# Scaling a recurrence's output by its root mean square: eight ScalarE operations one chunk later, or two VectorE operations behind the factor

## The chip, the cores and the metric

The kernel runs on one core of a Trainium2 chip. The metric is the time of one execution on the device, in microseconds (us). Three runs of the kernel before took 2665.38, 2669.21 and 2672.31 us; their median, 2669.21 us, is what the changed kernel is compared with.

## The reference, cut to what matters

One layer of a hybrid encoder: an input projection, a gated delta-rule recurrence over 8 heads of width 128, an attention group beside it, an output projection and a final norm. The sequence has 1024 frames of a new stream and 32 frames of a running one. The change lies in the recurrence and the norm that follows it:

```python
def step(s, xs):
    q_c, k_c, u_c, w_c, g_c, a_c = xs
    v_new = u_c - einsum('bhid,bhdv->bhiv', w_c, s)
    o_c = (einsum('bhid,bhdv->bhiv', q_c * exp(g_c)[..., None], s)
           + einsum('bhij,bhjv->bhiv', a_c, v_new))
    s = s * exp(g_last)[..., None, None] + einsum('bhid,bhiv->bhdv', k_dec, v_new)
    return s, o_c
...
o_g = rmsnorm(o_g, gdn_norm_w)      # per frame and head: o / sqrt(mean(o*o) + EPS) * w
o_g = o_g * silu(z_g)
```

## The kernel before

The program is a row of stages, each a block that all engines enter and leave together: `normalise_inputs`, `project`, `delta_rule` (with `decays`, `prepare` and `recur`), `attend`, and `mix_and_finish`. The change touches `recur` alone.

`recur` goes over NC = 9 chunks of 128 frames, c = 0 to 8; the last (LAST = 8) holds the 32 frames of the running stream, padded to 128. Its tensors have 128 partitions (frames of the chunk) and 8 heads of 128 columns. Work is cut in two halves g of HF = 4 heads, each one PSUM bank of 128x512. Every engine has its own list of instructions, written out by hand in program order, and does them strictly in that order; between engines stand semaphores (`then_inc`, `wait_ge`). So what is late on an engine is late for everything behind it on that engine.

In chunk c the order is, by engine (the names are those of the code):

- TensorE (PE): the keys times the state S (into banks 4 and 5, semaphore value kS); the form product of chunk c+1 from its loaded blocks (Bo, Xd); the triangular matrix times R (yP), which waits for R; the queries times the state (qS); the first peel of chunk c+1; the two products with y, for the new state (dS) and for o (Ay); `turn_out(c-1)`, which transposes the scaled o of the chunk before; the second peel; the transposes of the keys of c+1; the third peel; the transposes of the values of c+1.
- VectorE (DVE): R in eight operations of one head (L1070); a subtraction per peel (L1039); the new state S (L1080); the addition that completes o (L1085); `gated(c-1)`, which multiplies the transposed o by the gate and writes `mix` (L1054); `keys(c+1)` (L1046); in chunks 0 to 2 a share of 60 small operations that invert 32x32 blocks for chunks 4 to 7 (L576, L579); and then a chain for the norm: sum of squares `oss` (L1097), `var` (L1099, L1101), and, behind GpSimd, the factor `orr` (L1105). The next instruction on VectorE is R of chunk c+1.
- ScalarE (ACT): copies of the form product (L971), two copies of y (L1011), the queries' part of o (L998), then `normalise(c-1)`: eight operations of one head that scale o of the chunk before by `orr` (L988), `values(c+1)` into `vs` (L980), and the squares of o(c) (L1020).
- GpSimd (POOL): one power, var to the minus half (L962), and, in the chunks 1 to 6, ten small operations of its own inversion for the last chunk (`invert_steps`, L576 and L579 again), which stand in its list between the power of one chunk and that of the next.
- SyncE's queue (SP) issues the loads of the inputs, blocks and gates two chunks ahead, and the stores of `mix`. The blocks for chunk 4 wait until the inverse that VectorE made in chunks 0 to 2 has gone through DRAM.

o has two buffers, by the parity of c, while `orr`, `rms`, `var` and `oss` have one. Therefore VectorE waits for `normalise(c-1)` (`scaled`) before it writes `orr` of chunk c, and PE's `turn_out` waits for the same semaphore, `tail_s`. The counts by which the waits are written are lambdas: `squared` and `scaled`, and 4 increments of `stat` in each chunk.

Of the kernel before, what the change touches and what calls it, by code (L numbers as in the profile page):

```python
# [7 lines left out]
ACT = mybir.ActivationFunctionType  # L8
AX = mybir.AxisListType

P = 128
# [544 lines left out]
HF = HEADS // 2  # L556
# [248 lines left out]
def recur(nc, a, d, cols, ident, out, eg, egl, neg_eg, kl, root_q, root_k, sq2):  # L805
# [6 lines left out]
    with ExitStack() as ctx:  # L812
# [3 lines left out]
        LAST = PROMPT_TILES  # L816
        ROUNDS = NSUB - 1
        qkv = s.sb("qkv", [P, 2, 3 * HEADS, P])
        gate, mix, aT, Bo, Xd, Yd, V, o = (s.sb(n, [P, 2, HEADS, P]) for n in ("gate", "mix", "aT", "Bo", "Xd", "Yd", "V", "o"))
        S = s.sb("S", [P, 2, HEADS, P])  # L820
        pc, kd, vs, R, y, osq = (s.sb(n, full) for n in ("pc", "kd", "vs", "R", "y", "osq"))
        oss, var, rms, orr = (s.sb(n, [P, HEADS]) for n in ("oss", "var", "rms", "orr"))
# [6 lines left out]
        half = lambda g: slice(HF * g, HF * g + HF)  # L829
# [16 lines left out]
        formed = lambda c, g=1: 2 * (ROUNDS + 1) * c + g + 1  # L846
        peel_at = lambda c, r, g=1: 2 * (ROUNDS + 1) * c + 2 * r + g + 3
        y_at, qe_at = (lambda c, g=1, w=w: 4 * c + 2 * w + g + 1 for w in range(2))
        squared, scaled = (lambda c: 3 * c + 1), (lambda c, g=1: 3 * c + g + 2)
        RA, SA, OA = (lambda c, g=1, w=w: 6 * c + 2 * w + g + 1 for w in range(3))  # L850
        stream = lambda c: 1 if c == LAST else 0
        width = lambda c: DEC if c == LAST else P
# [88 lines left out]
        @block.gpsimd  # L941
        def _(pool):
            for t in (Xd, Yd, Bo):
                pool.memset(t[:], 0.0).then_inc(set_up, 1)
            pool.memset(S[:, 0], 0.0).then_inc(set_up, 1)
            pool.memset(mhalf[:], -0.5).then_inc(set_up, 1)
            pool.wait_ge(set_up, 5)
            pool.wait_ge(consts_in, 32)
            pool.wait_ge(sdiag_in, 16)
            invert_start(pool, sstep, Ls, Xs, below, HEADS)  # L950
            for c in range(NC):
                if 0 < c < 7:
                    invert_steps(pool, sstep, Ls, Xs, tmps, HEADS, 5 * c - 4, 5 * c + 1)
                if c == 6:
                    pool.wait_ge(sstep, INVERTED)
                    pool.tensor_copy(Ys[:].rearrange("p (j i) -> p j i", i=SUB), Xs[:].rearrange("p (i j) -> p j i", j=SUB)).then_inc(ys_turned, 1)
                    pool.wait_ge(V_s, level(6, ROUNDS - 1))
                    pool.memset(Yd[:, LAST % 2], 0.0).then_inc(sample_padded, 1)
                    pool.wait_ge(made, qS(LAST - 2))
                    pool.memset(qkv[:, LAST % 2, :, DEC:], 0.0).then_inc(sample_padded, 1)  # L960
                pool.wait_ge(stat, 4 * c + 3)
                pool.tensor_tensor(rms[:], var[:], mhalf[:], ALU.pow).then_inc(rms_s, 1)  # L962

        @block.scalar
        def _(act):
            def form(c):
                for g in range(2):
                    act.wait_ge(peeled, formed(c, g))
                    if c >= 1:
                        act.wait_ge(peeled, peel_at(c - 1, ROUNDS - 1, g))  # L970
                    act.copy(pc[:, half(g)], bank(g)).then_inc(pc_s, 1)  # L971

            def values(c):
                for g in range(2):
                    act.wait_ge(turned, vT(c, g))
                    if c >= 1:
                        act.wait_ge(rso, RA(c - 1, g))
                    for h in range(HF):
                        k = HF * g + h
                        last = act.activation(vs[:, k], bank(2 + g)[:, h], ACT.Copy, scale=root_k[:, c, k:k + 1])  # L980
                    last.then_inc(vs_s, 1)

            def normalise(c):
                act.wait_ge(stat, 4 * c + 4)
                for g in range(2):
                    for h in range(HF):
                        k = HF * g + h
                        last = act.activation(o[:, c % 2, k], o[:, c % 2, k], ACT.Copy, scale=orr[:, k:k + 1])  # L988
                    last.then_inc(tail_s, 1)

            def queries(c):
                for g in range(2):
                    act.wait_ge(made, qS(c, g))
                    if c >= 2:
                        act.wait_ge(oT, two(c - 2, g))
                    for h in range(HF):
                        k = HF * g + h
                        last = act.activation(o[:, c % 2, k], bank(4 + g)[:, h], ACT.Copy, scale=eg[:, c, k:k + 1])  # L998
                    last.then_inc(yq_s, 1)

            form(0)
            values(0)
            for c in range(NC):
                if c + 1 < LAST:
                    form(c + 1)
                for g in range(2):
                    act.wait_ge(made, yP(c, g))
                    if c >= 1:
                        act.wait_ge(made, Ay(c - 1, g))
                        act.wait_ge(made, dS(c - 1, g))  # L1010
                    act.copy(y[:, half(g)], bank(6 + g)).then_inc(yq_s, 1)  # L1011
                queries(c)
                if c >= 1:
                    normalise(c - 1)
                if c + 1 < NC:
                    values(c + 1)
                act.wait_ge(rso, OA(c))
                if c >= 1:
                    act.wait_ge(stat, 4 * (c - 1) + 1)
                act.activation(osq[:], o[:, c % 2], ACT.Square).then_inc(tail_s, 1)  # L1020
                if c == 2:
                    act.wait_ge(step, INVERTED)
                    act.copy(Y[:].rearrange("p (j i) -> p j i", i=SUB), X[:].rearrange("p (i j) -> p j i", j=SUB)).then_inc(y_turned, 1)
            normalise(LAST)

        @block.vector
        def _(dve):
# [34 lines left out]
            for c in range(NC):  # L1062
                for g in range(2):
                    dve.wait_ge(made, kS(c, g))
                    dve.wait_ge(vs_s, two(c, g))
                    if c >= 1:
                        dve.wait_ge(made, yP(c - 1, g))
                    for h in range(HF):
                        k = HF * g + h
                        last = dve.scalar_tensor_tensor(R[:, k], bank(4 + g)[:, h], neg_eg[:, c, k:k + 1], vs[:, k], ALU.mult, ALU.add)  # L1070
                    last.then_inc(rso, 1)
                if c + 1 < LAST:
                    peel(c + 1, 0)
                for g in range(2):
                    dve.wait_ge(made, dS(c, g))
                    if c >= 1:
                        dve.wait_ge(rso, SA(c - 1, g))
                    for h in range(HF):
                        k = HF * g + h
                        last = dve.scalar_tensor_tensor(S[:, stream(c), k], S[:, stream(c), k], egl[:, c, k:k + 1], bank(6 + g)[:, h], ALU.mult, ALU.add)  # L1080
                    last.then_inc(rso, 1)
                for g in range(2):
                    dve.wait_ge(made, Ay(c, g))
                    dve.wait_ge(yq_s, qe_at(c, g))
                    dve.tensor_tensor(o[:, c % 2, half(g)], o[:, c % 2, half(g)], bank(4 + g), ALU.add).then_inc(rso, 1)  # L1085
                if c + 1 < LAST:
                    peel(c + 1, 1)
                if c >= 1:
                    gated(c - 1)
                if c + 1 < NC:  # L1090
                    keys(c + 1)
                if c + 1 < LAST:
                    peel(c + 1, 2)
                if c < 3:
                    invert_steps(dve, step, L, X, tmp, P, (1, 11, 21)[c], (11, 21, 31)[c])
                dve.wait_ge(tail_s, squared(c))
                dve.tensor_reduce(oss[:], osq[:], AX.X, ALU.add).then_inc(stat, 1)  # L1097
                dve.wait_ge(stat, 4 * c + 1)
                dve.tensor_tensor(var[:], oss[:], sq2[:, c], ALU.mult).then_inc(stat, 1)  # L1099
                dve.wait_ge(stat, 4 * c + 2)  # L1100
                dve.tensor_scalar(var[:], var[:], EPS, None, ALU.add).then_inc(stat, 1)  # L1101
                dve.wait_ge(rms_s, c + 1)
                if c >= 1:
                    dve.wait_ge(tail_s, scaled(c - 1))
                dve.tensor_tensor(orr[:], rms[:], root_q[:, c], ALU.mult).then_inc(stat, 1)  # L1105
            gated(LAST)

        @block.tensor
        def _(pe):
# [45 lines left out]

            def turn_out(c):
                for g in range(2):
                    pe.wait_ge(tail_s, scaled(c, g))
                    if c + 1 < NC:
                        pe.wait_ge(vs_s, two(c + 1, g))  # L1160
                    turn(2, g, o[:, c % 2], oT)
# [1107 lines left out]
```

## Time and profile before

| | |
|---|---|
| median of three runs | 2669.21 us (2665.38 to 2672.31) |
| profiled execution, its own time | 2670.6 us |
| its span, first to last instruction | 2668.7 us |
| busy in the span: PE, DVE, ACT, POOL | 2288.1, 859.0, 657.6, 131.0 us |
| mean granted TensorE clock | 0.924 of full speed |
| `recur`, of that span | from about 1376 to 1678 us |

A row of a timeline gives the start in us from the span's start, the time it took, engine, line, operation, output and inputs, the number of operations merged (x), and in brackets the idle time of that engine before it and what ended it. A row of the operations by line gives count, busy time, mean in ns. Where an engine takes up the next operation while the former is still finishing, the rows overlap by some hundredths of a us.

### The profile page before, as it was taken

The numbers are of one execution on the slowest core, as the hardware profiler recorded it, in microseconds if no ns is written. First come the engines' busy times: TensorE is split into PE (matmuls) and PEld (weight loads), VectorE is DVE, ScalarE is ACT, GpSimd is POOL, SyncE is SP. The second block draws the span as 40 slices with busy tenths as digits, with TensorE's granted clock in tenths as the row PEclk, the third lists the DMA queues.
The fourth block names the chain that finished last, engine by engine and source line by source line (L and its number), as shares of the span: only waits on it lengthen the run. The fifth ranks groups of instructions, "written<-read, shape, count | busy, mean of one in ns | idle before, by whom it ended". The sixth has DMA issues, their size and how long they took to land. (4 is left out here: it accounts for less than half of the span.)

```text
span 2668.7 us, 35422 instructions
## 1 busy us (share of the span) xinstructions
PE 2288.1 (86%) x14534; PEld 2211.0 (83%) x14534; DVE 859.0 (32%) x1495; ACT 657.6 (25%) x1109; POOL 131.0 (5%) x192
## 2 busy tenths in 40 slices
PE   3799999999999999995846587379999977999991
PEld 3799999999999999994646576278998967999991
DVE  4233323332111111101535554445445442122114
ACT  7222222222111111112212333334333332111110
POOL 0000000000000000001331221000000000000000
PEclk8899999999999999996768788679999988999996
DMA  3221222222222222213556362331211124332327
GB/s 132 63 72 57 71 71 72 63 72 72 74 70 71 71 71 72 72 41 87 150 146 129 98 145 49 125 101 33 61 53 41 41 100 130 92 96 75 85 65 292
DMA packets 318743, 232.15 MB, mean 87 GB/s; under 512 B 56205, under 2 KB 299102, under 8 KB 315366
## 3 DMA queue, kind: packets, MB, share of 16 engines
q1 hardware_dynamic: 291750, 182.03, 24.7%
q10 hardware_dynamic: 26912, 49.01, 4.8%
q8 instruction: 55, 0.90, 0.1%
q14 instruction: 26, 0.21, 0.0%
HBM read 159.28 MB, written 67.40 MB: 85 GB/s over the span
## 5 line engine op out<-in xcount | busy, mean ns | idle before, releaser
L432 PE MATMUL proj_acc<-h_hn_hi,proj_w_hi 128*128 128x352 f32 (+1 forms) x2352 | 759.6, 323 | 12.3 <-DVE proj_w_lo L377 12.3
L432 PE MATMUL proj_acc<-h_hn_lo,proj_w_hi 128*128 128x352 f32 (+1 forms) x2352 | 754.7, 321 | 0.0
L432 PE MATMUL proj_acc<-h_hn_hi,proj_w_lo 128*128 128x352 f32 (+1 forms) x2352 | 754.2, 321 | 0.0
L432 PEld LDWEIGHTS proj_acc<-h_hn_hi,proj_w_hi 128*128 128x128 f32 (+1 forms) x2352 | 439.9, 187 | 13.2 <-DVE proj_w_lo L377 12.4
L432 PEld LDWEIGHTS proj_acc<-h_hn_lo,proj_w_hi 128*128 128x128 f32 (+1 forms) x2352 | 440.6, 187 | 0.8
L432 PEld LDWEIGHTS proj_acc<-h_hn_hi,proj_w_lo 128*128 128x128 f32 (+1 forms) x2352 | 439.5, 187 | 0.7
L377 DVE TENSOR_TENSOR proj_w_lo<-proj_w_raw,proj_w_hi 128x2048 fp32r<-128x2048 f32 (+1 forms) x49 | 111.5, 2277 | 588.0 <-ACT proj_w_hi L313 588.0
L2145 PE MATMUL mixo_acc<-mixo_m_hi,outw_w_hi 128*128 128x352 f32 x768 | 250.8, 327 | 35.3 <-DVE mixo_m_lo L2102 33.5
L2145 PE MATMUL mixo_acc<-mixo_m_hi,outw_w_lo 128*128 128x352 f32 x768 | 248.0, 323 | 0.0
L2145 PE MATMUL mixo_acc<-mixo_m_lo,outw_w_hi 128*128 128x352 f32 x768 | 247.6, 322 | 0.0
L2145 PEld LDWEIGHTS mixo_acc<-mixo_m_hi,outw_w_hi 128*128 128x128 f32 x768 | 145.1, 189 | 37.6 <-issue 18.9
L2145 PEld LDWEIGHTS mixo_acc<-mixo_m_lo,outw_w_hi 128*128 128x128 f32 x768 | 145.7, 190 | 0.0
L2145 PEld LDWEIGHTS mixo_acc<-mixo_m_hi,outw_w_lo 128*128 128x128 f32 x768 | 145.2, 189 | 0.0
L352 ACT ACTIVATE proj_act_out<-proj_acc 128x352 f32<-128x352 f32 x72 | 33.4, 464 | 445.9 <-PE proj_acc L432 445.9
L2092 DVE TENSOR_TENSOR mixo_yb<-mixo_back,mixo_xb 128x512 f32<-128x512 f32 (+1 forms) x48 | 23.6, 546 | 263.3 <-PE mixo_back L2132 263.3
L393 DVE TENSOR_SCALAR proj_act_out<-proj_pre,all_cols 128x1059 f32<-128x1059 f32 x24 | 18.5, 773 | 268.5 <-ACT proj_pre L342 268.5
L313 ACT CAST proj_w_hi<-proj_w_raw 128x2048 fp32r<-128x2048 f32 (+1 forms) x49 | 92.9, 1896 | 41.4 <-ACT proj_act_out L352 16.0
L397 DVE SCALAR_TENSOR_TENSOR proj_act_out<-proj_pre,all_cols,proj_act_out 128x1059 f32<-128x1059 f32 x72 | 95.2, 1323 | 10.7 <-DVE proj_act_out L393 3.6
L2040 ACT COPY mixo_yT<-mixo_acc 128x352 f32<-128x352 f32 x48 | 18.8, 460 | 324.0 <-PE mixo_back L2132 313.9
L1899 PE MATMUL mla_oT<-mla_pT,mla_v_tok 128*128 128x128 f32 (+2 forms) x624 | 83.9, 278 | 7.7 <-DVE mla_mix L1783 3.8
L1899 PEld LDWEIGHTS mla_oT<-mla_pT,mla_v_tok 128*128 128x128 f32 (+1 forms) x624 | 76.3, 191 | 13.1 <-issue 11.7
L1117 PE MATMUL rec_b<-rec_R,rec_V 128*128 128x128 f32 x128 | 28.4, 412 | 45.6 <-DVE rec_R L1070 45.6
(290 smaller groups left out, 3074.3 us busy)
## 6 DMA issues: line engine op xcount, KB each, us to landing
proj_w_raw<-in_w_in SPq DMA_DIRECT2D x48, 1024.0 KB, 5.6
outw_w_raw<-in_w_out SPq DMA_DIRECT2D x16, 1024.0 KB, 6.1
scratch_qkv<-proj_act_out ACTq DMA_DIRECT2D x24, 529.5 KB, 2.9
rec_qkv<-scratch_qkv SPq DMA_DIRECT2D x8, 1536.0 KB, 7.7
scratch_gate<-proj_act_out ACTq DMA_DIRECT2D x16, 528.0 KB, 2.7
mixo_m_lo<-scratch_mix SPq DMA_DIRECT2D x12, 704.0 KB, 11.3
norm_x<-in_x_prompt SPq DMA_DIRECT2D x8, 1024.0 KB, 5.0
prep_qk<-scratch_qkv SPq DMA_DIRECT2D x8, 1024.0 KB, 6.2
```

The costliest lines, as they stand in the source:

```text
L313: act.copy(w_hi[:, b, :, 0:n], w_raw[:, :, 0:n]).then_inc(hi_ready, 1)
L352: last = act.activation(act_out[:, b, NW * c:NW * c + NW], acc[b][c][:, 0:NW], ACT.Silu if kind == "gate" else ACT.Copy)
L377: dve.tensor_tensor(w_lo[:, b, :, 0:n], w_raw[:, :, 0:n], w_hi[:, b, :, 0:n].bitcast(F32), ALU.subtract).then_inc(lo_ready, 1)
L393: dve.tensor_scalar(y, pre[:, b, 0:CONV], w[0], None, ALU.mult).then_inc(conv_step, 1)
L397: ins = dve.scalar_tensor_tensor(y, pre[:, b, n:n + CONV], w[n], y, ALU.mult, ALU.add)
L432: last = pe.matmul(acc[b][c][0:n, 0:NW], w[:, b, k, 0:n], h[:, k, cut], start=(k == 0 and x == 0), stop=(k == KT - 1 and x == 2))
L1117: last = pe.matmul(bank(b + g)[:, h], lhsT[:, f], rhs[:, f], start=True, stop=True)
L1899: last = pe.matmul(oT[:, 0:n], v_tok[0:m, b, e], pT[0:m, (g - 3) % 2, P * j:P * j + n], start=(j == 0), stop=(j == len(parts) - 1))
L2040: act.copy(yT[:, NW * c:NW * c + NW], acc[u][c][:, 0:NW]).then_inc(yT_ready, 1)
L2092: dve.tensor_tensor(yb[0:rows, u, t0:t1], back[g % 2][0:rows, 0:P * (t1 - t0)].rearrange("p (t n) -> p t n", n=P), xb[0:rows, u, t0:t1], A ...
L2145: last = pe.matmul(acc[u][c][:, 0:NW], w[:, u, k], h[:, k, cut], start=(k == 0 and x == 0), stop=(k == KT - 1 and x == 2))
```

## The change

The eight ScalarE operations of `normalise` and both its calls go. In their place VectorE, right behind `orr` and still in chunk c, multiplies o in two operations of four heads each, in place, with the factor broadcast along the 128 columns of a head. Before them it waits for its own `orr`. `stat` now counts six increments in a chunk, `tail_s` one, and `turn_out` waits on `stat`. The wait of VectorE for `scaled(c-1)` goes.

```diff
-        squared, scaled = (lambda c: 3 * c + 1), (lambda c, g=1: 3 * c + g + 2)
+        squared, scaled = (lambda c: c + 1), (lambda c, g=1: 6 * c + g + 5)
...
-            def normalise(c):
-                act.wait_ge(stat, 4 * c + 4)
-                for g in range(2):
-                    for h in range(HF):
-                        k = HF * g + h
-                        last = act.activation(o[:, c % 2, k], o[:, c % 2, k], ACT.Copy, scale=orr[:, k:k + 1])
-                    last.then_inc(tail_s, 1)
...
                 queries(c)
-                if c >= 1:
-                    normalise(c - 1)
                 if c + 1 < NC:
                     values(c + 1)
...
-            normalise(LAST)
...
                 dve.wait_ge(rms_s, c + 1)
-                if c >= 1:
-                    dve.wait_ge(tail_s, scaled(c - 1))
                 dve.tensor_tensor(orr[:], rms[:], root_q[:, c], ALU.mult).then_inc(stat, 1)
+                dve.wait_ge(stat, 6 * c + 4)
+                for g in range(2):
+                    dve.tensor_tensor(o[:, c % 2, half(g)], o[:, c % 2, half(g)], orr[:, half(g), None].to_broadcast([P, HF, P]), ALU.mult).then_inc(stat, 1)
...
             def turn_out(c):
                 for g in range(2):
-                    pe.wait_ge(tail_s, scaled(c, g))
+                    pe.wait_ge(stat, scaled(c, g))
```

## Rows read from the trace of the kernel before

**Rows 1.** Timeline of all engines, from the squares of chunk 3 to chunk 4's first products
```profile
1545.92 1.10 ACT L1020 ACTIVATE rec_osq<-rec_o 128x1024 f32<-128x1024 f32 x1
...
1547.06 1.22 DVE L1097 TENSOR_REDUCE rec_oss<-rec_osq 128x8 f32<-128x1024 f32 x1 [2.90 <-ACT rec_osq L1020]
...
1548.31 0.17 DVE L1099 TENSOR_TENSOR rec_var<-rec_oss,gdn_sq 128x8 f32<-128x8 f32 x1
1548.52 0.17 DVE L1101 TENSOR_SCALAR rec_var<-rec_var 128x8 f32<-128x8 f32 x1
1548.77 1.64 POOL L962 TENSOR_TENSOR rec_rms<-rec_var,rec_mhalf 128x8 f32<-128x8 f32 x1 [28.70 <-DVE rec_var L1101]
1550.37 0.58 POOL L576 TENSOR_TENSOR rec_tmps<-rec_Ls,rec_Xs 8x240 f32<-8x240 f32 x1
1550.44 0.54 DVE L1105 TENSOR_TENSOR rec_orr<-rec_rms,gdn_root_q 128x8 f32<-128x8 f32 x1 [1.75 <-POOL rec_rms L962]
1550.90 2.15 DVE L1070 SCALAR_TENSOR_TENSOR rec_R<-rec_b,gdn_neg_eg,rec_vs 128x128 f32<-128x128 f32 x8
1551.03 0.69 POOL L579 TENSOR_TENSOR rec_Xs<-rec_Xs,rec_tmps 8x240 f32<-8x240 f32 x1
...
1552.07 3.78 PE L1117 MATMUL rec_b<-rec_R,rec_V 128*128 128x128 f32 x16 [4.19 <-DVE rec_R L1070]
...
1555.64 3.01 PE L1117 MATMUL rec_b<-rec_S,rec_qkv 128*128 128x128 f32 x16
```

**Rows 2.** Waits of `recur`: waiter, what it waited for, us in total, times, longest
```profile
ACT rec_vs L980 <- PE rec_b L1122: 69.2, 8, 9.5
```

**Rows 3.** Timeline of chunk 5: ScalarE's scaling of o, and PE's transposes of it
```profile
1587.35 2.47 ACT L988 ACTIVATE rec_o<-rec_o,rec_orr 128x128 f32<-128x128 f32 x8
...
1589.60 1.95 PE L1117 MATMUL rec_b<-rec_y,rec_aT 128*128 128x128 f32 x16
...
1591.39 1.04 PE L1122 MATMUL rec_b<-all_ident,rec_o 128*128 128x128 f32 x8
```

**Rows 4.** VectorE operations of this size in `normalise_inputs`: by tile (ns min/median/max), then timeline
```profile
L183 DVE TENSOR_TENSOR h_hn_lo<-norm_hn,h_hn_hi x36: 283/684/694, 20.2 to 79.3; 128x512 f32 x24, 128x512 fp32r<-128x512 f32 x8, 128x128 fp32r<-128x128 f32 x4
...
29.90 1.29 DVE L183 TENSOR_TENSOR h_hn_lo<-norm_hn,h_hn_hi 128x512 f32 x2
```

**Rows 5.** Timeline around the factor of chunk 6, where POOL has nothing behind its power
```profile
1633.22 0.17 DVE L1105 TENSOR_TENSOR rec_orr<-rec_rms,gdn_root_q 128x8 f32<-128x8 f32 x1 [1.75 <-POOL rec_rms L962]
1633.33 2.16 DVE L1070 SCALAR_TENSOR_TENSOR rec_R<-rec_b,gdn_neg_eg,rec_vs 128x128 f32<-128x128 f32 x8
...
1634.51 3.78 PE L1117 MATMUL rec_b<-rec_R,rec_V 128*128 128x128 f32 x16 [5.64 <-DVE rec_R L1070]
```

**Rows 6.** Line L1105, the factor: ns min/median/max over the nine chunks
```profile
L1105 DVE TENSOR_TENSOR rec_orr<-rec_rms,gdn_root_q x9: 166/353/539, 1449.7 to 1670.7; 128x8 f32<-128x8 f32 x9
```

**Rows 7.** Timeline: POOL's second operation behind its power, in chunks 0 and 5
```profile
1449.97 0.25 POOL L579 TENSOR_TENSOR rec_Xs<-rec_Xs,rec_tmps 8x30 f32<-8x30 f32 x1
...
1606.16 0.43 POOL L579 TENSOR_TENSOR rec_Xs<-rec_Xs,rec_tmps 8x130 f32<-8x130 f32 x1
```

**Rows 8.** Timeline, VectorE and PE, R and the form product of chunk 3
```profile
1513.82 2.15 DVE L1070 SCALAR_TENSOR_TENSOR rec_R<-rec_b,gdn_neg_eg,rec_vs 128x128 f32<-128x128 f32 x8
...
1523.53 3.77 PE L1117 MATMUL rec_b<-rec_Xd,rec_Bo 128*128 128x128 f32 x16 [18.01 <-DMA rec_Yd<-scratch_inv]
```

**Rows 9.** Timeline of the end of `recur`
```profile
1670.73 0.17 DVE L1105 TENSOR_TENSOR rec_orr<-rec_rms,gdn_root_q 128x8 f32<-128x8 f32 x1 [1.75 <-POOL rec_rms L962]
1670.93 2.45 ACT L988 ACTIVATE rec_o<-rec_o,rec_orr 128x128 f32<-128x128 f32 x8 [3.71 <-DVE rec_orr L1105]
...
1672.26 2.29 PE L1122 MATMUL rec_b<-all_ident,rec_o 128*128 128x128 f32 x8 [5.98 <-ACT rec_o L988]
...
1674.59 0.75 DVE L1054 SCALAR_TENSOR_TENSOR rec_mix<-rec_b,all_cols,rec_gate 128x512 f32<-128x512 f32 x1 [0.32 <-PE rec_b L1122]
1675.36 0.37 SPq L896 DMA_DIRECT2D scratch_mix<-rec_mix  x1
```

More of the change, by code:

```diff
@@ L960, in _ @@
                     pool.memset(qkv[:, LAST % 2, :, DEC:], 0.0).then_inc(sample_padded, 1)
-                pool.wait_ge(stat, 4 * c + 3)
+                pool.wait_ge(stat, 6 * c + 3)
                 pool.tensor_tensor(rms[:], var[:], mhalf[:], ALU.pow).then_inc(rms_s, 1)
@@ L1018, in _ @@
                 if c >= 1:
-                    act.wait_ge(stat, 4 * (c - 1) + 1)
+                    act.wait_ge(stat, 6 * (c - 1) + 1)
                 act.activation(osq[:], o[:, c % 2], ACT.Square).then_inc(tail_s, 1)
@@ L1097, in _ @@
                 dve.tensor_reduce(oss[:], osq[:], AX.X, ALU.add).then_inc(stat, 1)
-                dve.wait_ge(stat, 4 * c + 1)
+                dve.wait_ge(stat, 6 * c + 1)
                 dve.tensor_tensor(var[:], oss[:], sq2[:, c], ALU.mult).then_inc(stat, 1)
-                dve.wait_ge(stat, 4 * c + 2)
+                dve.wait_ge(stat, 6 * c + 2)
                 dve.tensor_scalar(var[:], var[:], EPS, None, ALU.add).then_inc(stat, 1)
                 dve.wait_ge(rms_s, c + 1)
-                if c >= 1:
-                    dve.wait_ge(tail_s, scaled(c - 1))
                 dve.tensor_tensor(orr[:], rms[:], root_q[:, c], ALU.mult).then_inc(stat, 1)
+                dve.wait_ge(stat, 6 * c + 4)
+                for g in range(2):
+                    dve.tensor_tensor(o[:, c % 2, half(g)], o[:, c % 2, half(g)], orr[:, half(g), None].to_broadcast([P, HF, P]), ALU.mult).then_inc(stat, 1)
             gated(LAST)
```

## The prediction

> **What bounds the kernel now.** I read the page first (busy shares, the 40 slices), then the timeline of all engines in the stretch of the recurrence, then the waits of that stretch, and last single lines and tiles for durations. Over the whole span PE is the busiest engine, but an average says nothing about `recur`, where no engine is busy all the time: what counts there is which wait ends last in each chunk.
>
> The timeline shows that this is the norm's own chain, although the next chunk doesn't need its result [rows 1]. ScalarE squares o until 1547.02. VectorE, idle for 2.90 us until then, sums the squares (1547.06, 1.22 us), does two small operations on `var` (1548.31 and 1548.52), waits for GpSimd's power (1548.77, 1.64 us), and makes the factor `orr` (1550.44). R of chunk 4 stands behind it in VectorE's list and starts at 1550.90. PE has then been idle for 4.19 us, and the row names R as what ended that. So whatever VectorE does between `orr` and R is on the path that sets the end, in each chunk where PE waits for R.
>
> ScalarE has time to spare. Before the values of the next chunk it waits for PE's transposes, 69.2 us in 8 waits, up to 9.5 us [rows 2].
>
> **What is removed.** Eight operations of ScalarE in each chunk, 2.47 us together [rows 3]. They lie between the queries' part of o and the values. In chunk 5 they run from 1587.35 to 1589.82, and PE takes the scaled o at 1591.39, right behind a product that started at 1589.60 and kept it busy. So nobody waits for them, and behind them ScalarE only waits longer for PE [rows 2]. I count their removal as 0, except in the last chunk. The dropped wait of VectorE for `scaled(c-1)` was over long before VectorE came to it: in chunk 5 the scaling ends at 1589.82, and GpSimd's operation that follows the factor of that chunk starts at 1606.16 [rows 3, 7]. So that is 0 as well. `turn_out` waits for a count reached about a chunk earlier: 0. No DMA is added or moved.
>
> **What is added, per chunk.** A wait of VectorE for its own factor, and two operations of 128x512 in place. This pair is not in the trace, but its nearest row is an operation of VectorE with two SBUF inputs of the same size: 684 ns, and two in a row take 1.29 us [rows 4]. The wait for an own result shows between the two operations on `var`: the second starts 0.21 us after the first, which took 0.17, so 0.04 us for the wait [rows 1]. Where nothing interferes, the factor starts at 1633.22, takes 0.17, and R starts 0.11 behind that start, which is 0.06 before the factor's end [rows 5]. With the pair R starts 0.17 + 0.04 + 1.29 - 0.06 = 1.44 us behind the start of the factor, so 1.33 us later. Queued behind it on VectorE are R's eight operations, and PE, then ScalarE's copies of y, wait for these. Nothing later in the chunk gives this back, because all of it follows from R.
>
> **How often this is on the path.** There are eight steps from a factor to the next R, and one of them is covered. In chunk 3 R started at 1513.82, but PE then waited until 1523.53 for the blocks of chunk 4 from DRAM (18.01 us idle, ended by a DMA), with its product of R behind that [rows 8]. Those blocks hang on VectorE's inversion in chunk 2, which ends before the pair of chunk 2. So there the pair costs 0. If the cover were gone it would cost the same 1.33. That leaves 7 x 1.33 = 9.3 us.
>
> **What GpSimd does to the pair.** In chunks 0 to 5 GpSimd goes on with its inversion right behind the power. The factor, the one operation of VectorE with two SBUF inputs there, takes 166 ns at least and 539 at most [rows 6]. The 0.17 belongs to a chunk in which GpSimd has nothing more to do [rows 5], and the 0.54 to one where GpSimd's operation runs from 1550.37 to 1550.95 and the factor ends at 1550.98 [rows 1]. So the factor is held until GpSimd's operation is over. GpSimd's next operation starts at 1551.03, 0.05 us behind the factor's end, and the first of the new pair would start at 1551.02 by the 0.04 above. I take it that VectorE comes first by that little, that GpSimd's second operation then stands waiting, and that it goes in between the two halves of the pair. It holds up the second half by its own length, in the five chunks 0, 1, 3, 4 and 5: the first of the five is 0.25 us, the last 0.43 [rows 7], the longest 0.69 [rows 1], and the sum of the five, with 0.48 and 0.58 for the two not shown, is 2.4 us. The bounds: 0 if GpSimd never gets in, and, if it comes first before both halves, the length of one more of its operations each time (0.59 in chunk 3's case, about 2.2 over the five), so 4.6 us. I take the middle, 2.4, since the factor's own row shows that the wait is real.
>
> The Trainium skill bears on this ("SBUF — State Buffer", section "Who interferes with whom"): a VectorE instruction with two SBUF inputs and a GpSimd instruction that reads SBUF exclude each other, and the one that issues second is blocked until the first ends. The factor's rows agree with it [rows 1, 6]. By that rule alone ScalarE's place for this scaling was the free one, and the pair pays for one or two of GpSimd's operations in each of these chunks, as in the sum or above it. The page doesn't say who is served when both are waiting.
>
> **The end of the stage.** Here the scaling is on the path. After the last factor ScalarE needs from 1670.93 to 1673.38, PE's eight transposes take 2.29 us from 1672.26, and the last of `mix` starts at 1674.59, with its store behind it at 1675.36 [rows 9]. The pair would run from 1670.94 to 1672.23, and GpSimd is idle. PE could start at 1670.94 + 0.68 + 0.04 = 1671.66, so 0.60 us earlier, if it needs the 2.29 us again. If it goes by the second half of o, that is there 1.15 us earlier. I take -0.9.
>
> **Sum.** 9.3 + 2.4 - 0.9 = +10.8 us. The profiled execution took 2670.6 us and would take 2681.4. It lies 1.4 above the median of the runs, so against the median of 2669.2 I predict 2680.0 us.
>
> **Rivals.**
> (a) No clash with GpSimd: VectorE's two halves follow each other without a gap. For it: they stand in VectorE's queue with no wait between them. Against it: the factor is held up in every chunk where GpSimd works on. 9.3 - 0.9 = +8.4, 2677.6 us.
> (b) GpSimd comes first twice. For it: the margin before the first half is 0.01 us, less than these rows can tell. 9.3 + 4.6 - 0.9 = +13.0, 2682.2 us.
> (c) The other side: the pair falls into time in which PE would wait anyway, as in chunk 3. It decides at 1.33 us of slack in R. Then only the end of the stage is left, -0.9 and 2668.3 us, not slower. For it: one step of eight is so [rows 8]. Against it: in the other chunks the row of PE's idle time names R [rows 1, 5], and VectorE is the engine that R stands behind.
> (d) The clock. PE comes back from its idle time slow: the 16 products of R take 3.78 us behind 4.19 idle, and 3.78 behind 5.64 idle [rows 1, 5], while 16 products at full clock take 1.95 [rows 3]. That the longer idle time changes nothing there is in my sum. The next 16, with the queries, took 3.01 [rows 1], between the two. If the added wait shifted them all to slow, each of the seven chunks would lose 3.78 - 3.01 = 0.77, in all +5.4: 2685.4 us. If all came at full clock, 7 x 1.06 = 7.4 would come back: 2672.6 us. I see nothing in the rows that favours a side.
>
> **How the numbers follow.** My forecast 0.45, (a) 0.27, (b) 0.13, (c) 0.05, (d) 0.10, half on each side. What a measurement of this kernel can tell from no change is about 0.3%, 8.0 us: up to 2677.2 counts as the same. The runs of before lie within 7 us, so I give each case some 2.5 us of spread. My forecast then falls under that line about 1 time in 8, (a) nearly half the time, (c) nearly always and (d) half the time, in all 0.26. Slower is 0.70, and 0.04 stays for faster, which no case gives by itself. The range from 2674 to 2685 holds (a), my forecast and (b) with their spread and leaves out (c) and the ends of (d).
>
> **What would show it.** In the changed trace R starts about 1.3 us later behind the factor than before in chunks 7 and 8, and 1.6 to 2.0 us later in chunks 1, 2, 4, 5 and 6. PE's idle time before R grows by as much, and doesn't in chunk 4's form product, which still waits for a DMA. ScalarE's line of the scaling is gone and its idle time before the values has grown by about 2.4 us. GpSimd's second operation behind the power starts late. If the two halves follow each other in 1.29 us everywhere, (a) holds. If PE's wait for R doesn't grow, (c) does and the forecast is wrong.

## The result: slower by 6 to 8 us, by the mechanism of the forecast and by less than its sum

Seven runs of the changed kernel had a median of 2675.93 us (2673.49 to 2678.66), seven of the kernel before beside them 2669.82: +6.1 us, ratio 1.0024 [1.0013, 1.0036]. A second set later (e4) gave 1.0030 [1.0019, 1.0040]. All 15 runs of the changed kernel together have a median of 2677.07, all 65 of the kernel before 2669.21: +7.9. The forecast was 2680.0, range 2674 to 2685. One run of e1 took 3501.86 us at a granted clock of 0.636 and is left out of every comparison.

The page of the changed kernel, part 1, its busy line (engine, us, share, instructions):

```profile
PE 2283.6 (85%) x14534; PEld 2206.0 (83%) x14534; DVE 872.3 (33%) x1513; ACT 635.6 (24%) x1037; POOL 135.9 (5%) x192
```

VectorE has 13.3 us more than before and ScalarE 22.0 less. Neither number is the change in time. That is read from the timeline. The changed kernel from the factor of chunk 3 to the first products of chunk 4, where [rows 1] stand:

```profile
1548.15 0.58 POOL L576 TENSOR_TENSOR rec_tmps<-rec_Ls,rec_Xs 8x240 f32<-8x240 f32 x1
1548.22 0.54 DVE L1092 TENSOR_TENSOR rec_orr<-rec_rms,gdn_root_q 128x8 f32<-128x8 f32 x1 [1.75 <-POOL rec_rms L962]
1548.79 1.79 DVE L1095 TENSOR_TENSOR rec_o<-rec_o,rec_orr 128x512 f32<-128x512 f32 x2
1548.81 1.22 POOL L579 TENSOR_TENSOR rec_Xs<-rec_Xs,rec_tmps 8x240 f32<-8x240 f32 x1
1550.11 0.93 POOL L576 TENSOR_TENSOR rec_tmps<-rec_Ls,rec_Xs 8x238 f32<-8x238 f32 x1
1550.51 2.15 DVE L1059 SCALAR_TENSOR_TENSOR rec_R<-rec_b,gdn_neg_eg,rec_vs 128x128 f32<-128x128 f32 x8
...
1551.68 3.76 PE L1107 MATMUL rec_b<-rec_R,rec_V 128*128 128x128 f32 x16 [6.00 <-DVE rec_R L1059]
...
1555.25 1.97 PE L1107 MATMUL rec_b<-rec_S,rec_qkv 128*128 128x128 f32 x16
```

The pair stands between factor and R, and R starts 2.29 us behind the factor's start instead of 0.46. PE's idle time before R's products has grown from 4.19 to 6.00. Two more things are to be seen. The pair took 1.79 us and not 1.29, while GpSimd's second operation took 1.22 instead of 0.69. And the queries' products behind R's took 1.97 us, where they had taken 3.01.

Where GpSimd has nothing to do, the factor of chunk 6 and R of chunk 7 (as [rows 5]):

```profile
1634.60 0.17 DVE L1092 TENSOR_TENSOR rec_orr<-rec_rms,gdn_root_q 128x8 f32<-128x8 f32 x1 [1.75 <-POOL rec_rms L962]
1634.80 1.29 DVE L1095 TENSOR_TENSOR rec_o<-rec_o,rec_orr 128x512 f32<-128x512 f32 x2
1636.01 2.15 DVE L1059 SCALAR_TENSOR_TENSOR rec_R<-rec_b,gdn_neg_eg,rec_vs 128x128 f32<-128x128 f32 x8
...
1637.19 3.68 PE L1107 MATMUL rec_b<-rec_R,rec_V 128*128 128x128 f32 x16 [6.92 <-DVE rec_R L1059]
```

R starts 1.41 us behind the factor's start, before 0.11. The covered step, R and the form product of chunk 3 (as [rows 8]):

```profile
1512.03 0.52 DVE L1092 TENSOR_TENSOR rec_orr<-rec_rms,gdn_root_q 128x8 f32<-128x8 f32 x1 [1.75 <-POOL rec_rms L962]
1512.59 1.71 DVE L1095 TENSOR_TENSOR rec_o<-rec_o,rec_orr 128x512 f32<-128x512 f32 x2
1514.22 2.15 DVE L1059 SCALAR_TENSOR_TENSOR rec_R<-rec_b,gdn_neg_eg,rec_vs 128x128 f32<-128x128 f32 x8
...
1521.67 3.42 PE L1107 MATMUL rec_b<-rec_Xd,rec_Bo 128*128 128x128 f32 x16 [17.48 <-DMA rec_Yd<-scratch_inv]
```

PE waits for the DMA as before. Its form product starts 7.5 us after R has begun (9.7 before). The end of the stage (as [rows 9]; the last row is the next stage's first load):

```profile
1674.37 0.17 DVE L1092 TENSOR_TENSOR rec_orr<-rec_rms,gdn_root_q 128x8 f32<-128x8 f32 x1 [1.75 <-POOL rec_rms L962]
1674.57 1.29 DVE L1095 TENSOR_TENSOR rec_o<-rec_o,rec_orr 128x512 f32<-128x512 f32 x2
...
1675.32 1.97 PE L1112 MATMUL rec_b<-all_ident,rec_o 128*128 128x128 f32 x8 [5.40 <-DVE rec_o L1095]
1676.57 1.51 DVE L1043 SCALAR_TENSOR_TENSOR rec_mix<-rec_b,all_cols,rec_gate 128x512 f32<-128x512 f32 x2 [0.70 <-PE rec_b L1112]
1678.10 0.37 SPq L896 DMA_DIRECT2D scratch_mix<-rec_mix  x1
...
1681.01 0.93 SPq L1258 DMA_DIRECT2D lat_raw<-scratch_latent  x2
```

From the factor to the store of `mix` it is 3.73 us; before it was 1675.36 - 1670.73 = 4.63.

The waits of `recur`, for PE, and then for ScalarE (waiter, what it waited for, us in total, times, longest), changed kernel:

```profile
PE rec_b L1107 <- DVE rec_R L1059: 61.8, 8, 12.6
```

```profile
ACT rec_vs L980 <- PE rec_b L1112: 85.3, 8, 11.9
```

PE's wait for R in the same view of the kernel before:

```profile
PE rec_b L1117 <- DVE rec_R L1070: 51.2, 8, 12.4
```

So PE waits 10.6 us longer for R, and ScalarE 16.1 longer for the transposes [rows 2]: most of the 22.0 us that it no longer works is waited there.

**The balance of the stage**, from chunk 0's R to the next stage's first load, is 256.25 us before and 261.36 after: +5.1. The steps from the factor to R, by chunk of the factor, are:

| | c0 | c1 | c2 (covered) | c3 | c4 | c5 | c6 | c7 |
|---|---|---|---|---|---|---|---|---|
| before | 0.11 | 0.33 | 0.45 | 0.46 | 0.42 | 0.46 | 0.11 | 0.11 |
| after | 1.50 | 1.94 | 2.19 | 2.29 | 2.14 | 1.85 | 1.41 | 1.41 |
| the pair's own time | 1.36 | 1.58 | 1.71 | 1.79 | 1.69 | 1.54 | 1.29 | 1.29 |

The seven steps that count add up to +10.54, and the end gives -0.90: +9.64, the sum on the path. The missing 4.5 lie on PE. From the start of R's products to the end of the queries', the eight other chunks took 50.21 us before and 46.67 after (-3.5), and in chunk 3 the wait for the DMA and the form product were 0.9 shorter, of which 0.4 is PE's pace. In the second set's profile (e4) the same stretch took 48.50 (-1.7), and the stage grew by 7.4. It fits chunk by chunk, too: from one R to the next the chunks 4 to 7 took 0.68, 1.63, 0.76 and 0.40 us longer than before, and the step together with the change in PE's two products gives 0.68, 1.65, 0.79 and 0.42.

Outside the stage the executions of all fourteen profiles differ by up to 6 us from that load to the end (988.9 to 994.8) and by up to 7.6 ahead of chunk 0's R (1417.0 to 1424.6), with no order by kernel. So the balance of the stage tells more than the total time of one profiled execution.

### The profile page after: what moved, and what is told of

Same layout as the page of the kernel before. It is cut to its first block and busy times, and to the rows that moved or that the text cites. A ratio compares the mean times of both kernels' runs of the same rounds, so it can differ in the third digit from the quotient of the medians.

```text
span 2672.2 us, 35360 instructions
## 1 busy us (share of the span) xinstructions
PE 2283.6 (85%) x14534; PEld 2206.0 (83%) x14534; DVE 872.3 (33%) x1513; ACT 635.6 (24%) x1037; POOL 135.9 (5%) x192
## 5 line engine op out<-in xcount | busy, mean ns | idle before, releaser
L1107 PE MATMUL rec_b<-rec_R,rec_V 128*128 128x128 f32 x128 | 27.9, 407 | 55.0 <-DVE rec_R L1059 55.0
```

The costliest lines, as they stand in the source:

```text
L1107: last = pe.matmul(bank(b + g)[:, h], lhsT[:, f], rhs[:, f], start=True, stop=True)
```

## The experiments

Two explanations of the missing 4.5 us. The clock: PE's products behind the longer wait come back to full speed sooner, and this pays part of the wait. The rival: taking eight operations a chunk from ScalarE frees time elsewhere, so that the pair costs more than was seen and the removal gives some back. A separate question is whether GpSimd really adds to the pair.

**e1: the pair alone, ScalarE's scaling kept.** The pair goes into `osq`, which nobody reads then. ScalarE's scaling and its next squares wait for it.

```diff
 # the kernel before, VectorE; the counts of stat change with it
 ...
                 dve.tensor_tensor(orr[:], rms[:], root_q[:, c], ALU.mult).then_inc(stat, 1)
+                dve.wait_ge(stat, 6 * c + 4)
+                for g in range(2):
+                    dve.tensor_tensor(osq[:, half(g)], o[:, c % 2, half(g)], orr[:, half(g), None].to_broadcast([P, HF, P]), ALU.mult).then_inc(stat, 1)
```

> The kernel before, with ScalarE's eight operations kept, and the pair of VectorE added behind the factor; the pair writes its product into the squares' buffer, where nobody reads it, so it is only time. Theory A (the pair is on the path, and ScalarE's operations were hidden except at the end): R starts 1.3 to 1.8 us later behind the factor, 10.5 us over the seven steps that count, nothing comes back at the end of the stage, and what the clock gives back (some 4 us in the profiled run of the changed kernel) comes back here too: +6 to +7 us against the kernel before, about 1 above the changed kernel. Theory B (ScalarE's removal itself is what made the change cheaper than the sum): ScalarE's operations are still here, so +10 to +11 us. Theory C (the pair falls into time that PE waits anyway): 0.

Measured: 2679.34 us (median of eight runs), ratio 1.0035 [1.0024, 1.0046], +10.0 by the medians. That lies nearer to the rival's number, but the expectation had overlooked the end of the stage, where ScalarE now waits for the pair too:

```profile
1680.64 0.17 DVE L1105 TENSOR_TENSOR rec_orr<-rec_rms,gdn_root_q 128x8 f32<-128x8 f32 x1 [1.75 <-POOL rec_rms L962]
1680.84 1.29 DVE L1108 TENSOR_TENSOR rec_osq<-rec_o,rec_orr 128x512 f32<-128x512 f32 x2
1682.17 2.45 ACT L988 ACTIVATE rec_o<-rec_o,rec_orr 128x128 f32<-128x128 f32 x8 [5.04 <-DVE rec_osq L1108]
```

From factor to store it is 5.96 us there, 2.2 more than in the changed kernel; without that, 7 to 8 would be left, beside the +6.1 and +7.9 of the whole change. So e1 does not tell the two explanations apart. It does show that the pair behaves the same while ScalarE keeps its work (within 0.02 us of the changed kernel's times in every chunk).

**e2: the changed kernel without the pair.** o is not scaled at all; only the counts of `stat` change with it.

```diff
 # the changed kernel, VectorE
 ...
-                dve.wait_ge(stat, 6 * c + 4)
-                for g in range(2):
-                    dve.tensor_tensor(o[:, c % 2, half(g)], o[:, c % 2, half(g)], orr[:, half(g), None].to_broadcast([P, HF, P]), ALU.mult).then_inc(stat, 1)
```

> The changed kernel without its pair: o isn't scaled at all, so the result of the recurrence group is left unscaled; the rest is as changed. Theory A: only the end of the stage gets shorter, there by all of the scaling, some 2.5 us, and the other chunks run as before: -2 to -3 us against the kernel before. Theory B (ScalarE's eight operations held something up in each chunk): some 0.5 us per chunk more, -6 us or below.

Measured: 2664.98 us, 0.9985 [0.9976, 0.9994], -4.4, between the numbers of the two theories. In its profile the stage is 2.8 shorter than before, of which the end is 1.6 (3.01 us from factor to store). The steps from factor to R are those of the kernel before, except 0.28 for 0.46 in chunk 5. The median fell by 1.6 us more than the stage, so medians differ by that much for reasons that the stage doesn't show.

**e7: the pair behind R of the next chunk.** The removal stays; the pair leaves the path, except in the last chunk.

```diff
 # the changed kernel, VectorE; scale(c) is the wait and the pair
                     last.then_inc(rso, 1)        # R of chunk c
+                if c >= 1:
+                    scale(c - 1)
...
+            scale(LAST)
             gated(LAST)
```

> The changed kernel with the pair moved behind R of the next chunk, where VectorE waits some 6 us for PE. Theory A (it is the place in VectorE's list that costs, not the operations): R starts as in the kernel before, 0.1 to 0.5 us behind the factor, the pair is hidden in all steps but the last, and the end keeps its gain of 0.9: -1 us against the kernel before, give or take 2 by the clock. If VectorE's busy time as such counted, or its clash with GpSimd further on, it would stay at +5 to +8.

Measured: 2667.43 us, 0.9996 [0.9987, 1.0005], -1.7. The steps from factor to R are short again (0.10 to 0.46), the end takes 3.74, and the stage is 2.0 shorter than before, 0.9 of it at the end; of the other 1.1, PE's pace makes 0.7. What the removal from ScalarE gives in the chunks is thus about 1 us or less, which these runs can't tell from nothing. So the rival can't be the cause of 4.5 us; e11 and e12 test it more sharply.

**e3: GpSimd's inversion waits until the pair is done.** **e4: the changed kernel once more**, in the same rounds.

```diff
 # e3: the changed kernel, GpSimd
                 if 0 < c < 7:
+                    pool.wait_ge(stat, 6 * c)
                     invert_steps(pool, sstep, Ls, Xs, tmps, HEADS, 5 * c - 4, 5 * c + 1)
```

> The changed kernel, in which GpSimd waits for the end of the pair of the chunk before it goes on with its inversion. Theory A: the pair takes 1.29 us in every chunk instead of 1.36 to 1.79, the factor 0.17 instead of 0.18 to 0.54, and R comes 0.1 to 0.9 us earlier in chunks 1, 2, 4, 5 and 6, about 2.5 us in all on the path, so 2 to 3 us faster than the changed kernel, +3 to +4 against before, if the clock behaves alike. If GpSimd is not what stretches these operations, their durations stay and so does the time.

> The changed kernel once more, for more runs and a second profile. VectorE's path gives 10.5 - 0.9 = +9.6 us; the first profile had 4 us less than that in PE's products behind the wait, which returned to full clock sooner. If that is what the longer wait brings, the median stays at +5 to +7 us and the second profile shows again shorter products of the queries (2.0 to 2.2 us in most chunks). If it was the luck of where the clock rose in that execution, the second profile shows others (2.3 to 3.1), and the medians over more runs go to +9 to +10.

Measured: e3 2670.99 us, 1.0008 [0.9999, 1.0017]; e4 2677.52, +8.15. This lies between the two cases of e4's expectation, and so does its profile: in the chunks 1, 2 and 4 to 8 three of the seven queries' products took 1.95 to 2.20 us and four 2.68 to 3.15. The timeline of e3, chunk 3 to 4:

```profile
1552.29 0.17 DVE L1093 TENSOR_TENSOR rec_orr<-rec_rms,gdn_root_q 128x8 f32<-128x8 f32 x1 [1.75 <-POOL rec_rms L963]
1552.49 1.29 DVE L1096 TENSOR_TENSOR rec_o<-rec_o,rec_orr 128x512 f32<-128x512 f32 x2
1553.70 2.15 DVE L1060 SCALAR_TENSOR_TENSOR rec_R<-rec_b,gdn_neg_eg,rec_vs 128x128 f32<-128x128 f32 x8
1553.86 0.58 POOL L576 TENSOR_TENSOR rec_tmps<-rec_Ls,rec_Xs 8x240 f32<-8x240 f32 x1 [1.61 <-DVE rec_o L1096]
```

Factor and pair take 0.17 and 1.29 here, as they do in all nine chunks of e3, and R starts 1.41 behind the factor's start everywhere. So it was GpSimd that stretched both. Over the seven steps that is 12.54 - 9.88 = 2.7 us, as expected. The time fell by 6.5, which is more. Part of the rest is PE's pace again; not all of it is settled (below).

**e5 and e6: PE kept busy ahead of R.** Both kernels get extra products (keys times state, into banks that the form product overwrites) in the time in which PE waits, so that its clock does not fall. The counts per chunk are 0, 3, 5, 0, 2, 2, 2, 3, 3 in the kernel before (e5) and 0, 4, 6, 0, 3, 3, 3, 3, 3 in the changed one (e6); each stands for eight products of the code, 16 in the rows.

```diff
 # PE, ahead of the form product
+                for n in range((0, 3, 5, 0, 2, 2, 2, 3, 3)[c]):
+                    for g in range(2):
+                        if n == 0:
+                            pe.wait_ge(V_s, level(min(c, LAST - 1), ROUNDS - 1, g))
+                        for h in range(HF):
+                            pe.matmul(bank(g)[:, h], part(c, 1)[:, HF * g + h], state[:, HF * g + h], start=True, stop=True)
                 if c + 1 < LAST:
                     form(c + 1)
```

> The kernel before, in which PE fills its wait for R with products into two PSUM banks that nobody reads then (2 to 5 times sixteen of them in chunks 1, 2 and 4 to 8, ahead of the form product), so that it isn't idle for more than some 0.5 to 1.8 us before R comes. Theory A says that the difference between the changed kernel and the sum of its parts (9.6 us) is TensorE's clock alone: the products of R and the queries then take 1.95 us each, as at full clock, instead of 3.78 and 2.3 to 3.1, which is 2.6 us per chunk in seven chunks, -18 us against the kernel before, with less spread between executions. If the slow products have another cause (the load of R as weights, PSUM), they stay at 3.78 and the time stays as before or grows a little.

> The changed kernel with PE's wait filled in the same way (3 to 6 times sixteen products, since the wait is longer). Theory A: with the clock out of the way the two kernels differ by VectorE's path and the end alone, 10.5 - 0.9 = +9.6 us above the kernel before with its wait filled, so some -8 us against the plain kernel before. Rival theory (what comes back in the changed kernel isn't the clock, but time that ScalarE's removal frees): the difference of the two filled kernels is again 6 to 8 us.

Measured: e5 2656.41 us, 0.9953 [0.9940, 0.9967]; e6 2661.57, 0.9974 [0.9965, 0.9983]. The expected gain of e5 was too large, in part because the counts left chunk 1 half slow (2.80 and 3.01 us for its two products; in e6 2.19 and 1.95). The two kernels lie 5.2 apart by the medians, below both numbers of e6's expectation, and 8.0 by the stage of their profiles. With chunks 0, 1 and 3 at different paces this is not yet the change alone.

**e11 and e12: the same with counts that keep every chunk from 1 on at full clock** (6, 4, 5, 9, 2, 2, 2, 3, 3 and 6, 4, 6, 9, 3, 3, 3, 3, 3).

> As the kernel before with PE's wait filled, but with all waits filled (6 and 4 times sixteen products in chunks 0 and 1, 9 in chunk 3), so that no product of the recurrence is slow. Theory A: 1.95 to 2.2 us for the products of R and of the queries in every chunk, 2 to 5 us less than in the kernel with five of the waits filled, -14 to -18 us against the kernel before.

> The changed kernel with all waits of PE filled. Theory A: nothing is left but VectorE's path and the end, 10.5 - 0.9 = +9.6 us above the kernel before with all waits filled; from the first product of R to the next stage's first load the profiles differ by 9 to 10 us, and the medians by that within the 2 to 3 us that the later stages spread. Rival theory: the difference stays at the 5 to 6 us of the two kernels filled before, so that something other than the clock takes back 4 us.

Measured: e11 2651.05 us, 0.9931 [0.9917, 0.9944]; e12 2659.32, 0.9963 [0.9950, 0.9977]. The timeline of e11 around R of chunk 5:

```profile
1572.61 2.15 DVE L1070 SCALAR_TENSOR_TENSOR rec_R<-rec_b,gdn_neg_eg,rec_vs 128x128 f32<-128x128 f32 x8
...
1573.78 2.19 PE L1117 MATMUL rec_b<-rec_R,rec_V 128*128 128x128 f32 x16 [0.57 <-DVE rec_R L1070]
...
1575.81 1.95 PE L1117 MATMUL rec_b<-rec_S,rec_qkv 128*128 128x128 f32 x16
...
1597.78 2.16 DVE L1070 SCALAR_TENSOR_TENSOR rec_R<-rec_b,gdn_neg_eg,rec_vs 128x128 f32<-128x128 f32 x8
```

And R of the chunks 5 and 6 in e12:

```profile
1578.19 2.15 DVE L1059 SCALAR_TENSOR_TENSOR rec_R<-rec_b,gdn_neg_eg,rec_vs 128x128 f32<-128x128 f32 x8
...
1604.75 2.15 DVE L1059 SCALAR_TENSOR_TENSOR rec_R<-rec_b,gdn_neg_eg,rec_vs 128x128 f32<-128x128 f32 x8
```

With 0.57 us idle ahead of it instead of 4.14, R's product takes 2.19 us instead of 3.78, and the queries' 1.95, the same in chunks 1, 2 and 4 to 7 of both kernels. The granted clock over these two is 1.00, in e12 as well. So the slow products were slow by the clock, and not by the load of R as weights. The changed kernel then costs 8.3 us by the medians, and its stage is 247.94 against 238.63: +9.3, where the path sum says +9.6. From R to R the chunks 4 to 7 are 1.71, 1.39, 1.29 and 1.30 us longer in e12 than in e11 (chunk 5 takes 26.56 instead of 25.17), and the steps of the path sum are 1.72, 1.39, 1.30 and 1.30. With the clock out of play 0.3 us of the sum is missing, which is all that is left for the rival. Both profiles are of the slowest of five runs, and the extra time lies outside the stage: from the next stage's first load to the end it is 994.8 and 991.3 us.

**e8, e9 and e10: the whole norm behind R.** The chain from `oss` on moves behind the next chunk's R, in the changed kernel (e8, and again as e10) and in the kernel before, with ScalarE's scaling kept (e9).

```diff
 # VectorE; norm(c) is the chain from the wait for squared(c) to orr (e8, e10: and the pair)
                     last.then_inc(rso, 1)        # R of chunk c
+                if c >= 1:
+                    norm(c - 1)
...
+            norm(LAST)
             gated(LAST)
```

> The changed kernel with the whole chain of the norm (sum of squares, the two operations on var, the wait for the power, the factor and the pair) moved behind R of the next chunk. Theory A (this chain is what PE waits for in each chunk): R starts as soon as the values are there, some 4 to 6 us earlier in the chunks 4 to 8 and about 3.5 earlier in 1 and 2, PE hardly waits and stays at full clock, which gives 2.6 more per chunk; against that the chain of 5 to 6 us now holds up VectorE's next subtraction by 1 to 2 us. Sum some -5 us per chunk in seven chunks: -25 to -45 us against the kernel before. If R is held by something else just behind the chain (the values, the keys' product), the gain is below 10 us.

> The kernel before, with ScalarE's eight operations kept, and VectorE's chain of the norm up to the factor moved behind R of the next chunk. With the chain off the path the two places for the scaling should differ by the end of the stage (0.9 us in favour of VectorE) and by the 0.45 us by which VectorE's next subtraction starts late behind the pair, at most 0.45 in each of five chunks in favour of ScalarE. Theory A: the same as the changed kernel with the chain behind R, -45 us against the kernel before, within 2 us. Rival: ScalarE's operations now are in the way, since a chunk has got 7 us shorter; then some 0.3 to 2.5 us more per chunk, +2 to +15 above the other.

> The changed kernel with the whole chain behind R once more, on the same chip and in the same rounds as the one with ScalarE's scaling: again -45 us against the kernel before, within 2 us.

Measured: e8 2624.16 us, 0.9837 [0.9823, 0.9850]; e10 2626.03, 0.9835 [0.9822, 0.9848]; e9 2623.78, 0.9832 [0.9818, 0.9845]. The timeline of e8, chunk 5:

```profile
1555.73 2.16 DVE L1072 SCALAR_TENSOR_TENSOR rec_R<-rec_b,gdn_neg_eg,rec_vs 128x128 f32<-128x128 f32 x8 [1.08 <-PE rec_b L1112]
...
1557.81 1.21 DVE L1048 TENSOR_REDUCE rec_oss<-rec_osq 128x8 f32<-128x1024 f32 x1
...
1558.21 1.95 PE L1112 MATMUL rec_b<-rec_R,rec_V 128*128 128x128 f32 x16
...
1561.70 1.69 DVE L1057 TENSOR_TENSOR rec_o<-rec_o,rec_orr 128x512 f32<-128x512 f32 x2
```

R now waits only for PE's own product, and PE goes through R's products without idle time, at full clock. From R to R a chunk takes 20.58 us in chunks 4 to 6 (before 27.1 to 27.7). All three beat both kernels by 43 us or more. In this place these runs don't tell whether ScalarE or VectorE scales o: e9 and e10 lie 2.3 us apart, and their runs overlap.

## Why the prediction came out as it did, step by step

**What bounds the stage: right.** PE's wait for R grew by 10.6 us, the seven steps by 10.54. Moving the pair behind R (e7) takes the cost away, moving the whole chain (e8) far more.

**The removal at 0, except at the end: right.** e7 bounds it at about 1 us, and e11 and e12 leave 0.3.

**The pair at 1.33 a step: right.** It is 1.30 where GpSimd is idle, 9.1 for the seven.

**Chunk 3 covered: right.** R is 1.74 us later behind its factor there, and PE still waited for the DMA.

**The end at -0.9: right**, 4.63 to 3.73. PE's transposes took 1.97 instead of 2.29 us.

**GpSimd's share of 2.4: the place right, the size too large.** VectorE came first, and GpSimd's second operation went in between the halves, in each of chunks 0 to 5, as the rows show. But it adds 1.44 to the five steps, since it costs the pair less than its own length: 0.07 of 0.25, 0.25 of 0.43 and 0.50 of 0.69 us, some 0.18 less each time. The rule of the Trainium skill ("SBUF — State Buffer", section "Who interferes with whom") agrees with these rows but for this 0.18, and e3 shows it by removal: without GpSimd's operations beside it the pair takes 1.29 us in every chunk. What its rule left open, who is served when both wait, the rows answer for this case: each in turn.

**"That the longer idle time changes nothing there is in my sum": this step failed, in size.** It is the term of rival (d), which I had split evenly for want of a row. What the runs show are the queries' products behind the wait, in the seven chunks that count by the path sum (R of the chunks 1, 2 and 4 to 8; us):

| profile | c1 | c2 | c4 | c5 | c6 | c7 | c8 | mean |
|---|---|---|---|---|---|---|---|---|
| before | 2.37 | 3.11 | 3.01 | 2.81 | 2.68 | 2.77 | 2.31 | 2.72 |
| e2, no scaling | 2.24 | 3.04 | 3.14 | 2.87 | 2.80 | 2.83 | 2.35 | 2.75 |
| e7, pair behind R | 2.10 | 2.97 | 3.06 | 2.83 | 2.78 | 2.82 | 2.34 | 2.70 |
| after | 1.95 | 1.97 | 1.97 | 3.07 | 2.16 | 1.95 | 2.87 | 2.28 |
| e4, after again | 3.02 | 2.68 | 2.13 | 3.15 | 2.20 | 1.95 | 2.88 | 2.57 |
| e1, pair added | 1.95 | 2.08 | 2.77 | 1.95 | 3.15 | 2.40 | 3.12 | 2.49 |
| e3, no clash | 3.04 | 2.93 | 2.58 | 2.09 | 1.95 | 1.95 | 2.77 | 2.47 |

The three with the short wait are all slower in the mean than the four with the pair ahead of R: 2.70 to 2.75 against 2.28 to 2.57. Not every chunk shows it, and chunk 8 shows the reverse. The granted clock says why chunk 4 was faster. The trace's windows over R's products and then over the queries' of chunk 4, changed kernel (window, length, busy us and count of PE, PEld, DVE, ACT, POOL, then the granted clock):

```profile
1551.70:1555.20 3.50, 3.50 (x16) 3.50 (x17) 0.95 (x4) 0.59 (x1) 3.03 (x7) 0.50 0.00 0
1555.30:1557.20 1.90, 1.90 (x19) 1.90 (x19) 0.00 (x0) 1.42 (x5) 0.50 (x1) 1.00 0.00 0
```

And the kernel before, the same two:

```profile
1552.10:1555.60 3.50, 3.50 (x16) 3.50 (x17) 0.94 (x4) 0.59 (x1) 3.11 (x6) 0.50 0.00 0
1555.70:1558.60 2.90, 2.90 (x18) 2.90 (x18) 0.00 (x0) 1.59 (x5) 1.30 (x3) 0.63 0.00 0
```

In both R's products run at 0.50, which is 1.2 GHz. In the changed kernel the queries' run at 1.00, 2.4 GHz, all through; before they ran at 0.63, so at the lower level most of the time. Counted from the start of R's products, the clock was back at 2.4 GHz after 3.6 us in the one and after 5.8 in the other. PE was idle for 6.00 us ahead in the one and 4.19 in the other. That this is what the sum lacks, and not a gain elsewhere, rests on e11 and e12: with PE busy ahead of R, the change costs its path sum within 0.3 us.

The corrected sum is 9.1 + 1.4 - 0.9 = 9.6 us on the path, less what the clock gives back: 4 in the first profile, 2 in the second. The pooled medians (+7.9) ask for about 2. The two errors of the prediction, 1.0 us in GpSimd's share and 2 to 4 in the clock, have the same sign, and its range was wide enough for both. By the line that it drew at 2677.2 us the first set would even count as the same, a case that it had given 0.26; the interval of the ratio, 1.0013 to 1.0036, doesn't hold 1, though. Rival (a)'s number, 2677.6, came nearer to the time than mine, but its mechanism is refuted: the pair was stretched in every chunk where GpSimd worked.

**Still open.** The length of the wait doesn't set when the clock returns. Chunk 4 has 6.00, 6.01 and 6.01 us idle in after, e4 and e1; the clock was back 3.6, 3.9 and 5.3 us after R's products began, and the queries took 1.97, 2.13 and 2.77. After 5.6 us idle they took 2.77 in chunk 7 before, 2.16 in chunk 6 after and 3.15 in chunk 6 of e1. So what is shown is that the queries' time follows the moment at which the clock rises, and that in these profiles this moment came earlier in the mean with the pair on the path; that a longer wait does this as such is not shown. The four readings of one profile aren't independent, either: before, in e2 and in e7 the chunks 4 to 7 follow each other in a nearly even rhythm (27.1 to 27.9 us from R to R), and the clock is back 5.1 to 6.1 us after R's products began in each of them. How the chunks of a kernel fall into it, and so how much of the 2 to 4 us another kernel would get, these runs don't tell.

Nor is all of e3 explained. Its path is 7.88 - 0.9 = +7.0 against before, and its PE took 2.7 less in the eight chunks, which fits its stage (+4.1), but its median is only 1.6 above before. Its profile is of the slowest of its eleven runs, 7.1 above their median, so it may not show what the others did.

## What to carry to other kernels

On an engine that goes through its list in order, as VectorE did here, what counts is not how much work it has but what stands ahead of the instruction that others wait for: moving 2.5 us of scaling a chunk from an engine with time to spare to that place cost 6 to 8 us, and moving the chain that nobody needs yet behind it gave 43 to 46. Look for such a chain before choosing which engine runs its last link. When a wait ahead of TensorE grows, count the wait and the pace of the products behind it separately, and where the pace matters, price the change once with TensorE kept busy, so that the clock doesn't blur the sum.

## What the runs showed of the hardware that was not expected

- VectorE's pair (two SBUF inputs each) and GpSimd's operations on SBUF beside it took turns, and both paid: the pair 1.29 to 1.79 us, GpSimd's two operations beside it 0.69 to 1.22 and 0.59 to 0.93. VectorE's loss was some 0.18 us less than the length of the operation let in.
- A longer idle time ahead of TensorE's products didn't cost more of their pace: R's 16 products took at most 3.79 us behind 4.0 to 14 us of idle time, and the 16 behind them 1.95 to 3.15, as the granted clock rose earlier or later. In the mean of the seven chunks these took 2.72 us before, and 2.28 and 2.57 in the two profiles of the changed kernel.
- Useless products in TensorE's idle time made the kernel before faster by 18 us (e11), since 32 products behind the wait then took 3.98 us in the chunks 1, 2 and 4 to 7 and not 5.95 to 6.68.
